# Hybrid decoder step: VectorE adds a slot's index pairs before it biases the slot's score

## The chip, the cores and the metric

The kernel runs on one core of a Trainium2 chip. The metric is the device time of one execution in microseconds (us). The kernel before took 6667.58 us, the median of 3 runs (6666.86 to 6669.77).

The engines of a core that matter here: PE (TensorE, matmuls; PEld is its weight load), VectorE (DVE), ScalarE (ACT), and SP, which issues the DMAs. Each works through its own list of instructions in order and waits on semaphores for the others.

## The reference

One layer of a decoder with three attention branches over one input projection. The branch that matters here is B, sparse attention with a learned choice of keys (DSA): 4096 prompt tokens, 6 heads of 64, 8 indexer heads; each query attends to the 256 keys of highest index score.

```
dots  = einsum('nthd,nsd->ntsh', qi, ki) * IDX_DIM ** -0.5
score = einsum('ntsh,nth->nts', relu(dots), wi) * IDX_HEADS ** -0.5     # 8 indexer heads, weighted and summed
score = where(key <= query, score, -inf)
_, sel = top_k(score, 256)
s = einsum('ntkgd,ntjkd->ntkgj', q, k[sel]) * HEAD_DIM ** -0.5
o = einsum('ntkgj,ntjkd->ntkgd', softmax(s), v[sel])
```

## The kernel before

Six stages run one after the other: memory projection, token projection, window attention, sparse attention for the prompt (`attend_sparse`), attention of the sampled tokens, and output projection. The change lies in `attend_sparse`.

It goes through 32 tiles of 128 queries. Instead of gathering keys it computes all scores of a tile against all keys up to it and adds a `bias` of -1e30 at keys that aren't selected. Keys are taken in chunks of up to 512. A *slot* is one head of a tile (n) and one chunk (g); tile t has 6 x (t // 4 + 1) of them. Three streams of work are interleaved over the slots:
- the attention of tile t: a score matmul into PSUM (PE, L980), biasing it into `p_S` with its running extreme in `p_mc` (VectorE, `biased`, L1131), the exponentials (ScalarE, L1046), and two heads later the transposes (PE, L1006), their copies to `p_PT` (ScalarE, L1054) and the product with the values (PE, L1016)
- the index scores of tile t + 2: an index matmul for one indexer head and one chunk (an *item*, PE, L989), its ReLU into one of three `relu` buffers (ScalarE, L1063), and, when a pair of chunks is there, an add of the weighted pair to `p_X` over up to 1024 columns (VectorE, `add_index`, L1161 for the first head and L1164 for the others). `index_share` deals the items evenly to the slots, one or two each for the most part, so that about two slots in three have an add
- the search for the 256th largest index score of tile t + 1: 14 *parts* (`parts_here`, `part`), dealt evenly to the slots of tile t. Eight of them count how many scores lie above a trial value (L1198) and work out the next one in small operations; the others centre, mask, take the next eight, and write the new bias (L1242). Most pass over the whole row of the tile.

Score and index matmuls share four PSUM banks `SC`, which are used in turn in the order in which PE issues them. Before PE writes a bank it waits for whoever reads it out: for a score VectorE's `biased`, for an item ScalarE's ReLU (`bank`, L967). That order is PE's own per slot: transposes of two heads ago, score, items, values. ScalarE's is: copies of transposes, exponentials of the head before, ReLUs. VectorE's order per slot is the loop that the change touches: bias, inverse of a head's softmax sum (first slot of a head), adds, search parts, and at a tile's end `finish`, which looks whether the search has found all rows.

The adds of the last two tiles do not exist (there is no tile 32 or 33), and there are no parts in tile 0.

Of the kernel before, what the change touches and what calls it, by code (L numbers as in the profile page):

```python
# [747 lines left out]
def attend_sparse(nc, ins, outs, scr):  # L748
# [6 lines left out]
    def n_chunks(t):  # L755
        return t // 4 + 1
# [7 lines left out]
    def tile_of(n):  # L764
        return n // HEADS

    def slots_of(n):
        qk = n_chunks(tile_of(n)) if n < NH else 0
        return max(qk, n_chunks(tile_of(n - LOOK)) if n >= LOOK else 0)

    def index_items(t):

        return [(h, big, c) for big in range((n_chunks(t) + 1) // 2) for h in range(8)
                for c in range(2 * big, min(2 * big + 2, n_chunks(t)))]
# [13 lines left out]
    def index_share(n, g):  # L788

        t = n // HEADS + 2  # L790
        if t >= NT:
            return []
        s, ns = place[n, g]
        items = index_items(t)
        return [(t, k) for k in range(len(items) * s // ns, len(items) * (s + 1) // ns)]

    def parts_here(n, g):

        t = n // HEADS + 1
        if not 2 <= t < NT:  # L800
            return []
        s, ns = place[n, g]
        return [i for i in range(PARTS) if (i * (ns - 1) // PARTS if i < PARTS - 1 else ns - 1) == s]
# [5 lines left out]
    def ends_here(n, g):  # L809
        s, ns = place[n, g]  # L810
        return 2 <= n // HEADS + 1 < NT and s == ns - 1
# [10 lines left out]
    for n in range(NH + LOOK):  # L822
        for g in range(slots_of(n)):
# [6 lines left out]
            if asks_here(n, g):  # L830
                t = n // HEADS + 1
# [3 lines left out]
    with ExitStack() as ctx:  # L835
# [277 lines left out]
        def _(dve):  # L1113
# [10 lines left out]
            def biased(n, g):  # L1124
                t, p = tile_of(n), n % 2
                w, r = width(t, g), ring["B", n, g]
                if g == 0 and n >= 3:
                    dve.wait_ge(p_turned, first_chunk[n - 2])
                dve.wait_ge(s_ready, r + 1)
                cols = slice(512 * g, 512 * g + w)  # L1130
                dve.tensor_tensor_reduce(S[:, n % 3, cols], SC[r % 4][:, 0:w], bias[:, cols], -SCALE, -FAR,  # L1131
                                         ALU.add, ALU.min, mc[:, p, g:g + 1]).then_inc(s_biased, 1)
                if g == n_chunks(t) - 1:
                    if n >= 2:
                        dve.wait_ge(exp_done, first_exp[n - 1])
                    dve.wait_ge(s_biased, first_chunk[n + 1])
                    dve.tensor_scalar(mjunk[:, p, 0:g + 1], mc[:, p, 0:g + 1], 1.0, None, ALU.mult, ALU.min,  # L1137
                                      accum_out=negm[:, p:p + 1]).then_inc(max_ready, 1)

            def inverse(n):  # L1140
                p, pieces = n % 2, first_exp[n + 1] - first_exp[n]
                dve.wait_ge(exp_done, first_exp[n + 1])
                dve.tensor_scalar(ljunk[:, 0:pieces], lparts[:, p, 0:pieces], 1.0, None, ALU.mult, ALU.add,
                                  accum_out=lsum[:, p:p + 1]).then_inc(l_summed, 1)
                if n >= 2:
                    dve.wait_ge(o_out, n - 1)
                dve.wait_ge(l_summed, n + 1)
                dve.reciprocal(linv[:, p:p + 1], lsum[:, p:p + 1]).then_inc(inv_ready, 1)

            def add_index(t, k):  # L1150
                h, big, cc = index_items(t)[k]
                if cc != min(2 * big + 1, n_chunks(t) - 1):
                    return
                a, b = 1024 * big, min(1024 * (big + 1), P * (t + 1))
                j = first_sum[t] + 8 * big + h
                x, r, w = X[:, t % 2, a:b], relu[:, j % 3, 0:b - a], iw[:, t % 2, h:h + 1]
                if k == 0:
                    dve.wait_ge(iq_in[t % 2], 80 * (t // 2))
                dve.wait_ge(relu_done, first_item[t] + k + 1)
                if h == 0:  # L1160
                    dve.scalar_tensor_tensor(x, r, w, ties[:, a:b], ALU.mult, ALU.add).then_inc(idx_added, 1)  # L1161
                else:
                    dve.wait_ge(idx_added, j)
                    dve.scalar_tensor_tensor(x, r, w, x, ALU.mult, ALU.add).then_inc(idx_added, 1)  # L1164
# [79 lines left out]
            def all_seen():  # L1244

                dve.wait_ge(s_biased, first_chunk[HEADS])
                dve.memset(bias[:, 0:P], 0.0)
                dve.tensor_copy(bias[:, P:2 * P], causal[:, :]).then_inc(passed, 1)
                dve.wait_ge(passed, 2)

            def part(t, i):
                if i == 0:
                    centre(t)
                elif i == 1:
                    begin(t)
                elif i < 2 + COUNTS:
                    count(t, i - 2)
                else:
                    (mask, next_eight, take, make_bias)[i - 2 - COUNTS](t)
# [40 lines left out]
            def finish(t):  # L1300

                dve.wait_ge(s_ready, ring["U", t] + 1)
                dve.sem_inc(passed, 1)
                link(dve.tensor_copy(undone[:, :], SC[ring["U", t] % 4][0:1, 0:1]))
                dve.sem_inc(told, 1)
                left = dve.value_load(undone[0:1, 0:1], min_val=0, max_val=P)
                before = done[0]
                with dve.If(left > 0):
                    search_all(t)
                    dve.sem_inc(passed, 1)  # L1310
                assert done[0] - before == SLOW_STEPS, done[0] - before
                with dve.Else():
                    dve.sem_inc(step, SLOW_STEPS)
                dve.wait_ge(step, done[0])
                dve.sem_inc(picked, 1)
                assert done[0] == STEPS * (t - 1), (done[0], t)
# [3 lines left out]
            dve.wait_ge(passed, 1)  # L1320
            for n in range(NH + LOOK):
                for g in range(slots_of(n)):
                    if n < NH and g < n_chunks(tile_of(n)):
                        biased(n, g)
                    if g == 0 and n >= LOOK:
                        inverse(n - LOOK)
                    for t, k in index_share(n, g):
                        add_index(t, k)
                    for i in parts_here(n, g):
                        part(n // HEADS + 1, i)  # L1330
                    if ends_here(n, g):
                        finish(n // HEADS + 1)
                    if (n, g) == slots[0][-1]:
                        all_seen()
# [851 lines left out]
```

## Time and profile before

| | |
|---|---|
| runs | 6666.86, 6667.58, 6669.77 us |
| profiled execution | 6669.09 us, span 6667.2 us |
| PE busy | 5927.4 us, 89% of the span |
| VectorE busy | 3641.5 us, 55% |
| ScalarE busy | 2845.0 us, 43% |
| mean granted TensorE clock | 0.953 |

Busy time is an average over stages with different limits. The sparse stage lies between about 2604 and 5870 us. The granted clock is given as a share of TensorE's full clock. A wait is the idle time of an engine in front of an instruction, with the instruction that ended it.

### The profile page before, as it was taken

The page shows a single profiled execution, that of the slowest core. Times are in us where ns is not written, and L with a number is a line of the kernel's source. Part 1 is how long each engine was busy: PE and PEld are TensorE (multiplying, and loading weights), DVE is VectorE, ACT ScalarE, POOL GpSimd, SP SyncE. Part 2 cuts the span into 40 slices and gives each one's busy share as a digit, 9 for nine tenths or more (in the row PEclk, how much of TensorE's full clock was granted, in tenths as well). Part 3 has the DMA queues.
Part 4 walks back from the last instruction along what each step waited for, and adds up shares of the span by engine and source line. Part 5 has one row for each costly group of instructions (what it writes and reads, how often), then busy time and mean ns, then how long its engine had stood idle before and what let it go on. Part 6 is the DMA issues. An engine that isn't in the chain of part 4 may idle for free. (4 is left out here: it accounts for less than half of the span.)

```text
span 6667.2 us, 78452 instructions
## 1 busy us (share of the span) xinstructions
PE 5927.4 (89%) x25717; PEld 3521.4 (53%) x25717; DVE 3641.5 (55%) x9535; ACT 2845.0 (43%) x6063; POOL 91.9 (1%) x172
## 2 busy tenths in 40 slices
PE   5999999999899996778888989888988888987998
PEld 2444444444566764445555556555555556743444
DVE  1111111111355555888888888777877777363554
ACT  1222222222354554455556665655655555521332
POOL 0000000000000000000000000000000000000000
PEclk8999999999899998799999999999999999998999
DMA  3111111111500003011100000000000000032443
GB/s 129 42 49 48 44 54 42 50 48 39 152 30 27 35 27 97 25 41 32 28 8 12 12 6 6 12 6 6 6 6 6 6 3 4 14 130 95 151 155 123
DMA packets 215242, 301.89 MB, mean 45 GB/s; under 512 B 38114, under 2 KB 169890, under 8 KB 213730
## 3 DMA queue, kind: packets, MB, share of 16 engines
q1 hardware_dynamic: 202514, 256.85, 12.1%
q0 software_dynamic: 12368, 40.71, 1.6%
q8 instruction: 168, 2.75, 0.2%
q14 instruction: 192, 1.57, 0.1%
HBM read 189.98 MB, written 120.08 MB: 47 GB/s over the span
## 5 line engine op out<-in xcount | busy, mean ns | idle before, releaser
L453 PE MATMUL t_zp<-t_w,t_xT 128*128 128x512 f32 (+1 forms) x3696 | 1442.6, 551 | 42.5 <-DVE t_w L406 42.5
L989 PE MATMUL p_SC<-p_ikT,p_iq 128*128 128x512 f32 (+3 forms) x2272 | 1125.0, 600 | 302.3 <-DVE p_mc L1131 301.4
L1016 PEld LDWEIGHTS p_OP<-p_bv,p_PT 128*128 128x128 f32 x6336 | 881.5, 200 | 396.9 <-issue 352.9
L453 PEld LDWEIGHTS t_zp<-t_w,t_xT 128*128 128x128 f32 x3696 | 662.2, 192 | 778.1 <-issue 735.2
L1063 ACT ACTIVATE p_relu<-p_SC 128x512 f32<-128x512 f32 (+3 forms) x1136 | 628.3, 565 | 750.0 <-PE p_SC L989 647.8
L980 PE MATMUL p_SC<-p_bkT,p_bq 128*128 128x512 f32 (+3 forms) x1728 | 860.7, 581 | 60.1 <-DVE p_mc L1131 59.8
L989 PEld LDWEIGHTS p_SC<-p_ikT,p_iq 128*128 128x128 f32 x2272 | 430.8, 200 | 865.9 <-DVE p_mc L1131 467.2
L1016 PE MATMUL p_OP<-p_bv,p_PT 128*128 128x64 f32 x6336 | 844.3, 277 | 10.1 <-ACT p_PT L1054 9.9
L1131 DVE CUSTOM_DVE_ANT_0 p_S<-p_SC,p_bias 128x512 f32<-128x512 f32 (+3 forms) x864 | 553.1, 645 | 311.7 <-PE p_SC L980 245.4
L288 ACT ACTIVATE t_z<-t_zp,t_rstd 128x512 f32<-128x512 f32 (+1 forms) x231 | 146.6, 635 | 1309.8 <-PE t_zp L453 1309.8
L1164 DVE SCALAR_TENSOR_TENSOR p_X<-p_relu,p_iw,p_X 128x1024 f32<-128x1024 f32 (+7 forms) x546 | 608.3, 1114 | 175.8 <-ACT p_relu L1063 167.1
L1054 ACT ACTIVATE p_PT<-p_TP 128x512 f32<-128x512 f32 (+3 forms) x864 | 485.4, 562 | 480.1 <-PE p_TP L1006 478.4
L1198 DVE TENSOR_SCALAR_CACHE_REDUCE p_Y<-p_X,p_col 128x384 bf16<-128x384 f32 (+29 forms) x240 | 609.6, 2540 | 1.0 <-issue 0.3
L1046 ACT ACTIVATE p_S<-p_S,p_negm 128x1024 f32<-128x1024 f32 (+7 forms) x480 | 477.8, 996 | 138.7 <-DVE p_mjunk L1137 101.3
L1006 PE MATMUL p_TP<-p_ident,p_S 128*128 128x128 f32 x3168 | 513.0, 282 | 18.9 <-ACT p_S L1046 18.8
L710 ACT ACTIVATE w_S<-w_S,w_o 128x256 f32<-128x256 f32 (+1 forms) x704 | 338.7, 482 | 416.7 <-DVE w_o L676 416.7
L2062 PE MATMUL f_zp<-f_w,f_mixT 128*128 128x512 f32 x1056 | 470.9, 605 | 0.0
L1006 PEld LDWEIGHTS p_TP<-p_ident,p_S 128*128 128x128 f32 x3168 | 400.0, 162 | 27.4 <-ACT p_S L1046 20.8
L685 DVE COPY w_PT<-w_TP 128x512 f32<-128x512 f32 (+1 forms) x352 | 226.6, 644 | 263.6 <-PE w_TP L620 263.2
L638 PEld LDWEIGHTS w_OP<-w_v,w_PT 128*128 128x128 f32 x2052 | 250.6, 191 | 158.5 <-DVE w_PT L685 158.5
L2062 PEld LDWEIGHTS f_zp<-f_w,f_mixT 128*128 128x128 f32 x1056 | 203.6, 196 | 244.9 <-issue 244.9
L386 DVE COPY t_qT<-t_tp 128x512 f32<-128x512 f32 (+1 forms) x132 | 81.4, 654 | 447.8 <-PE t_tp L439 447.2
(250 smaller groups left out, 5312.1 us busy)
## 6 DMA issues: line engine op xcount, KB each, us to landing
scr_qkT<-t_qT SPq DMA_DIRECT2D x33, 960.0 KB, 3.7
scr_part<-w_o POOLq DMA_DIRECT2D x96, 198.0 KB, 2.2
f_part<-scr_part SPq DMA_DIRECT2D x32, 594.0 KB, 4.7
t_x<-in_x_prompt SPq DMA_DIRECT2D x32, 512.0 KB, 3.7
f_gate<-scr_gate SPq DMA_DIRECT2D x32, 512.0 KB, 7.3
f_x<-in_x_prompt SPq DMA_DIRECT2D x32, 512.0 KB, 3.3
out_y_p<-f_y POOLq DMA_DIRECT2D x32, 512.0 KB, 6.5
p_iq<-scr_qkT SPq DMA_DIRECT2D x120, 128.0 KB, 2.8
```

Source lines behind the costliest of these rows:

```text
L453: mm = pe.matmul(zp[(NZ * p + c) % 2][:, 0:n], xT[:, p, k, :], w[:, k, a:a + n], start=(k == 0), stop=(k == KD - 1))
L980: pe.matmul(bank(ring["B", n, g])[:, 0:w], bq[:, t % 2, n % HEADS, :], bkT[:, 512 * g:512 * g + w], start=True, stop=True).then_inc(s_read ...
L989: pe.matmul(bank(ring["I", t, k])[:, 0:w], iq[:, t % 2, h, :], ikT[:, 512 * c:512 * c + w], start=True, stop=True).then_inc(s_ready, 1)
L1006: mm = pe.transpose(TP[m % 2][:, b, :], S[:, n % 3, c0:c0 + P], ident[:, :])
L1016: mm = pe.matmul(OP[n % 2][:, 0:HD], PT[:, m % 2, b, :], bv[:, 4 * g + b, s * HD:(s + 1) * HD], start=(g == 0 and b == 0), stop=(last and ...
L1046: act.activation(S[:, n % 3, a:b], S[:, n % 3, a:b], ACT.Exp, scale=-1.0, bias=negm[:, p:p + 1], accum_out=lparts[:, p, big:big + 1]).then ...
L1054: act.activation(PT[:, m % 2, 0:nb, :], TP[m % 2][:, 0:nb, :], ACT.Copy).then_inc(pT_ready, 1)
L1063: act.activation(relu[:, j % 3, 512 * (c % 2):512 * (c % 2) + w], SC[r % 4][:, 0:w], ACT.Relu, scale=0.5)\
L1131: dve.tensor_tensor_reduce(S[:, n % 3, cols], SC[r % 4][:, 0:w], bias[:, cols], -SCALE, -FAR, ALU.add, ALU.min, mc[:, p, g:g + 1]).then_in ...
L1164: dve.scalar_tensor_tensor(x, r, w, x, ALU.mult, ALU.add).then_inc(idx_added, 1)
L1198: link(dve.tensor_scalar(G[:, 0:L], X[:, t % 2, 0:L], c(W + 1), None, ALU.is_gt, ALU.add, accum_out=c(CNT)))
L2062: mm = pe.matmul(zp[2 * p + i][:, :], mixT[:, p, k * P:(k + 1) * P], w[:, k, i * 512:(i + 1) * 512], start=(k == 0), stop=(k == KD - 1))
```

## The change

In VectorE's loop over the slots the adds come ahead of the bias and the inverse; parts and the rest stay behind them.

```
             for n in range(NH + LOOK):
                 for g in range(slots_of(n)):
+                    for t, k in index_share(n, g):
+                        add_index(t, k)
                     if n < NH and g < n_chunks(tile_of(n)):
                         biased(n, g)
                     if g == 0 and n >= LOOK:
                         inverse(n - LOOK)
-                    for t, k in index_share(n, g):
-                        add_index(t, k)
                     for i in parts_here(n, g):
                         part(n // HEADS + 1, i)
```

The lists of the other engines stay as they are. On VectorE, in tile 23 (keys up to 3200 are counted for tile 24), between two counts that stand two slots apart, the kernel before has:

```order
L1223 SCALAR_TENSOR_TENSOR p_col<-p_col,p_signs 128x2
L1131 ISA p_S,p_mc<-p_SC,p_bias 128x512
L1131 ISA p_mc 128x1
L1164 SCALAR_TENSOR_TENSOR p_X<-p_relu,p_iw,p_X 128x1024
L1131 ISA p_S,p_mc<-p_SC,p_bias 128x512
L1131 ISA p_mc 128x1
L1137 TENSOR_SCALAR p_mjunk,p_negm<-p_mc 128x6
L1164 SCALAR_TENSOR_TENSOR p_X<-p_relu,p_iw,p_X 128x1024
L1198 TENSOR_SCALAR p_Y,p_col<-p_X,p_col 128x3200
```

The same place in the changed kernel (L1223 is the end of one count, L1198 the start of the next):

```order
L1223 SCALAR_TENSOR_TENSOR p_col<-p_col,p_signs 128x2
L1164 SCALAR_TENSOR_TENSOR p_X<-p_relu,p_iw,p_X 128x1024
L1131 ISA p_S,p_mc<-p_SC,p_bias 128x512
L1131 ISA p_mc 128x1
L1164 SCALAR_TENSOR_TENSOR p_X<-p_relu,p_iw,p_X 128x1024
L1131 ISA p_S,p_mc<-p_SC,p_bias 128x512
L1131 ISA p_mc 128x1
L1137 TENSOR_SCALAR p_mjunk,p_negm<-p_mc 128x6
L1198 TENSOR_SCALAR p_Y,p_col<-p_X,p_col 128x3200
```

Behind the first count the add (L1164) now precedes the bias (L1131); in front of the second count the bias and the head's extreme (L1137) now stand between add and count.

Behind that second count the next slot has no add, and is the first of a head. In the kernel before VectorE has there:

```order
L1223 SCALAR_TENSOR_TENSOR p_col<-p_col,p_signs 128x2
L1131 ISA p_S,p_mc<-p_SC,p_bias 128x512
L1131 ISA p_mc 128x1
L1143 TENSOR_SCALAR p_ljunk,p_lsum<-p_lparts 128x3
L1148 RECIPROCAL p_linv<-p_lsum 128x1
L1131 ISA p_S,p_mc<-p_SC,p_bias 128x512
L1131 ISA p_mc 128x1
L1164 SCALAR_TENSOR_TENSOR p_X<-p_relu,p_iw,p_X 128x1024
```

And in the changed kernel, at the same place:

```order
L1223 SCALAR_TENSOR_TENSOR p_col<-p_col,p_signs 128x2
L1131 ISA p_S,p_mc<-p_SC,p_bias 128x512
L1131 ISA p_mc 128x1
L1143 TENSOR_SCALAR p_ljunk,p_lsum<-p_lparts 128x3
L1148 RECIPROCAL p_linv<-p_lsum 128x1
L1164 SCALAR_TENSOR_TENSOR p_X<-p_relu,p_iw,p_X 128x1024
L1131 ISA p_S,p_mc<-p_SC,p_bias 128x512
L1131 ISA p_mc 128x1
```

The bias behind the count stays first, and only in the slot after it do add and bias change places.

## Rows read from the trace of the kernel before

**Rows 1.** VectorE's timeline (start, us long, instruction): where tiles 11 and 21 end.
```profile
3239.24 1.02 DVE L1242 TENSOR_SCALAR p_bias<-p_Y 128x1664 bf16<-128x1664 f32 x1
...
4165.78 1.62 DVE L1242 TENSOR_SCALAR p_bias<-p_Y 128x2816 bf16<-128x2816 f32 x1
```

**Rows 2.** Busy us (and instructions) of each engine, granted clock, DMA, by stretch.
```profile
2604.00:3239.00 635.00, 496.68 (x2118) 310.65 (x2117) 535.87 (x1820) 327.00 (x723) 0.00 (x0) 0.89 0.14 39
3239.00:4166.00 927.00, 834.70 (x3970) 534.22 (x3968) 769.96 (x1822) 553.99 (x1015) 0.00 (x0) 0.96 0.04 11
4166.00:5575.00 1409.00, 1261.09 (x5975) 810.47 (x5974) 1074.62 (x2140) 819.99 (x1417) 0.00 (x0) 0.96 0.02 7
```

**Rows 3.** PE's waits (total us, times, longest) in these three stretches, in turn.
```profile
PE p_SC L989 <- DVE p_mc L1131: 106.1, 50, 5.2
PE p_SC L980 <- DVE p_mc L1131: 16.0, 7, 7.7
...
PE p_SC L989 <- DVE p_mc L1131: 86.3, 57, 4.1
PE p_SC L980 <- DVE p_mc L1131: 5.8, 9, 1.2
...
PE p_SC L989 <- DVE p_mc L1131: 109.0, 61, 4.1
PE p_SC L980 <- DVE p_mc L1131: 34.2, 25, 2.5
```

**Rows 4.** PE's waits from 2604 to 5575 us, the next largest.
```profile
PE p_TP L1006 <- ACT p_S L1046: 18.8, 8, 4.8
```

**Rows 5.** VectorE's waits from 2604 to 5575 us, for ReLUs.
```profile
DVE p_X L1164 <- ACT p_relu L1063: 167.1, 192, 2.9
```

**Rows 6.** Timeline from 4500 us: start, us long, engine, instruction [idle before <- who ended it].
```profile
4500.77 0.69 DVE L1131 CUSTOM_DVE_ANT_0 p_S<-p_SC,p_bias 128x512 f32<-128x512 f32 x1 [3.20 <-PE p_SC L980]
...
4502.32 1.28 DVE L1164 SCALAR_TENSOR_TENSOR p_X<-p_relu,p_iw,p_X 128x1024 f32<-128x1024 f32 x1 [0.85 <-ACT p_relu L1063]
...
4503.52 3.54 DVE L1198 TENSOR_SCALAR_CACHE_REDUCE p_Y<-p_X,p_col 128x3200 bf16<-128x3200 f32 x1
4503.57 1.88 PE L989 MATMUL p_SC<-p_ikT,p_iq 128*128 128x512 f32 x4
...
4504.98 1.17 ACT L1063 ACTIVATE p_relu<-p_SC 128x512 f32<-128x512 f32 x2 [0.29 <-issue]
...
4506.57 1.02 PE L980 MATMUL p_SC<-p_bkT,p_bq 128*128 128x512 f32 x2
...
4508.80 0.69 DVE L1131 CUSTOM_DVE_ANT_0 p_S<-p_SC,p_bias 128x512 f32<-128x512 f32 x1
...
4509.42 1.28 DVE L1164 SCALAR_TENSOR_TENSOR p_X<-p_relu,p_iw,p_X 128x1024 f32<-128x1024 f32 x1
...
4509.56 3.33 PE L989 MATMUL p_SC<-p_ikT,p_iq 128*128 128x512 f32 x4 [1.97 <-DVE p_mc L1131]
```

**Rows 7.** VectorE's groups in the three stretches, in turn: count | busy, mean ns | idle.
```profile
L1164 DVE SCALAR_TENSOR_TENSOR p_X<-p_relu,p_iw,p_X 128x1024 f32<-128x1024 f32 (+7 forms) x126 | 122.6, 973 | 11.6 <-ACT p_relu L1063 8.1 <-issue 1.0 <-DVE p_X L1164 0.5
...
L1131 DVE CUSTOM_DVE_ANT_0 p_S<-p_SC,p_bias 128x512 f32<-128x512 f32 (+3 forms) x144 | 85.0, 590 | 47.3 <-PE p_SC L980 23.1 <-DVEq L1313 10.1 <-PE p_TP L1006 4.8
...
L1164 DVE SCALAR_TENSOR_TENSOR p_X<-p_relu,p_iw,p_X 128x1024 f32<-128x1024 f32 (+7 forms) x176 | 198.5, 1128 | 50.2 <-ACT p_relu L1063 47.7
...
L1131 DVE CUSTOM_DVE_ANT_0 p_S<-p_SC,p_bias 128x512 f32<-128x512 f32 (+3 forms) x252 | 161.2, 641 | 49.7 <-PE p_SC L980 25.6 <-DVEq L1313 17.6 <-DVE p_col L1203 1.1
...
L1164 DVE SCALAR_TENSOR_TENSOR p_X<-p_relu,p_iw,p_X 128x1024 f32<-128x1024 f32 (+7 forms) x245 | 288.3, 1177 | 114.8 <-ACT p_relu L1063 112.1
...
L1131 DVE CUSTOM_DVE_ANT_0 p_S<-p_SC,p_bias 128x512 f32<-128x512 f32 (+3 forms) x372 | 242.8, 658 | 136.6 <-PE p_SC L980 122.4 <-DVEq L1313 6.5 <-DVE p_col L1203 1.8
```

**Rows 8.** ScalarE's waits from 2604 to 5575 us, for a free ReLU buffer.
```profile
ACT p_relu L1063 <- DVE p_X L1164: 83.3, 53, 3.9
```

More of the change, by code:

```diff
@@ L1322, in _ @@
                 for g in range(slots_of(n)):
+                    for t, k in index_share(n, g):
+                        add_index(t, k)
                     if n < NH and g < n_chunks(tile_of(n)):
@@ L1326, in _ @@
                         inverse(n - LOOK)
-                    for t, k in index_share(n, g):
-                        add_index(t, k)
                     for i in parts_here(n, g):
```

## The prediction, made before the changed kernel ran

> **What bounds the kernel now.** I looked first for the stretch that the edit can reach: only the DSA stage (`attend_sparse`), and in it only tiles whose slots carry index work, that is from 2604 us to 5575 us, 2971 us of the span of 6667.2 us. The bias table of a tile is written at the end of the tile before; two of these ends cut the stretch in three [rows 1]: tiles 0 to 11, 12 to 21, and 22 to 29. Then I asked what each engine does there [rows 2]: PE is busy for 78, 90 and 90% of the three, VectorE for 84, 83 and 76%. Neither is idle enough to be out of the question, and neither is full: they hold each other up.
>
> Where, the waits tell. PE waits for `p_mc` of L1131, the biasing of a score, because the score's PSUM bank comes free only with it: 122.1 us in 57 waits, 92.1 in 66 and 143.2 in 86 [rows 3], 357 us in 209 waits. PE's only other wait of note, on ScalarE's exponentials, is 18.8 us [rows 4]. VectorE for its part waits 167.1 us for ReLUs in front of its adds [rows 5]. So the clock of the stage is a loop: PE fills the four banks, VectorE must bias a score to free one, and PE starts only as far ahead as the ring allows.
>
> One turn of that loop is in [rows 6]. At 4500.77 VectorE biases a score as soon as it is there. At 4502.32 it adds the slot's pair, 0.85 us after it ran dry, when the ReLU is done. From 4503.52 it counts (3.54 us, then eight small operations) and comes back at 4508.80. Meanwhile PE has done the next slot's score and two items (from 4503.57), and the score of the slot after (from 4506.57), and is stuck for 1.97 us until the bias of 4508.80 frees a bank at 4509.4; its item starts at 4509.56. Both ReLUs of that next slot were done at 4506.15 (4504.98 + 1.17), so at 4508.80 bias and add were both possible, and the kernel takes the one PE waits for.
>
> **The change, part by part.** No instruction is added or removed and no DMA is issued by VectorE here; PE's, ScalarE's and SP's lists are the same. In each of the 582 slots that by `index_share` have both a score and an add, the bias moves behind the add; with it moves the inverse of a softmax sum, in the first slot of a head. Two things follow around each search part.
>
> *Next slot.* After a part VectorE now adds first if the next slot has an add. In the turn above the add's step is 4503.52 - 4502.32 = 1.20 us: PE's bank comes free that much later.
>
> *Own slot.* If the slot of the part has an add itself, the bias that used to run while the ReLU was made now stands between add and part: 4509.42 - 4508.80 = 0.62 us. The part starts and ends that much later.
>
> For this turn both hold: 1.97 us become about 3.8. Now count them. The formulas of `index_share` and `parts_here` give, for the three stretches, 118, 140 and 112 slots with a part; 98, 100 and 86 of these have an add of their own; behind 99, 100 and 66 the next slot has one. With the mean durations of [rows 7] (bias 590, 641, 658 ns; add 973, 1128, 1177 ns):
> - tiles 0 to 11: 98 x 0.590 + 99 x 0.973 = 154 us
> - tiles 12 to 21: 100 x 0.641 + 100 x 1.128 = 177 us
> - tiles 22 to 29: 86 x 0.658 + 66 x 1.177 = 134 us
>
> 465 us would be it if every part held PE up. PE waited 57, 66 and 86 times for 118, 140 and 112 parts, 48, 47 and 77%, so 74, 83 and 103 us. In the first stretch nearly every slot has a part (118 in 138 slots), VectorE is the busiest engine, and an engine that sets the pace itself loses nothing by another order of work that is ready: I take half, 37 us. Waits: 37 + 83 + 103 = 223 us. Bounds: 0 (all hidden behind VectorE's own work) and 465.
>
> *Slots without a part.* In the 298 others with an add the bias goes from the moment the score is there to after ReLU and add; in the turn above from 4500.77 to 4503.52, when PE's next items want to start at 4503.57: about 0.6 us late if they need just that bank. Bounds 0 and 298 x 0.62 = 185 us; I take 0, since these slots are the ones in which the ring had room, and what PE waits there it waits less at the next part.
>
> *The clock.* After the wait of 1.97 us the two items took 3.33 us, against 1.88 us for the two before [rows 6]: half speed, the 1.2 GHz level against 2.4. The granted clock is 0.89 in the first stretch, where PE's waits are thickest (122.1 us in 635), and 0.96 in the two others (235.3 us in 2336) [rows 2, 3]. If these two fell all the way to 0.89, PE's 2095.8 busy us there would grow by 0.96/0.89, 165 us; if nothing changed, 0. No row shows how far it falls with 186 us more of waits. I take a fall to 0.93, a little under half of the way: 2095.8 x (0.96/0.93 - 1) = 68, of which I keep 60, since VectorE sets the pace part of the time. In the Trainium skill, "TensorE: Matmul & The Clock Gate", section "A second HAM failure mode: psum-queue depth-cycling", a kernel that cycles through PSUM banks with short idle spells between its matmuls swings between the two clock levels and loses throughput by it; the trace agrees, with the 3.33 us against 1.88.
>
> *Sum.* 223 + 60 = 283 us on the profiled execution's 6669.09 us (1.9 around the span) is 6952; that execution was 1.5 us over the median of the runs, so 6950 us.
>
> **Rivals.**
> *The order is hidden.* The same work is done by the same engine, bias and add are both ready behind a part, and VectorE is busy for some 80%. If it is the pace-setter throughout, PE's longer waits cost nothing: 6667.6 us, or up to 90 us more with the late tiles alone. For it: the first stretch. Against it: in tiles 22 to 29 VectorE is busy for only 76% and 86 of 112 parts do hold PE up. A rule of the Trainium skill points this way ("Perfetto Trace Analysis", section "Matmuls"): let matmul groups rotate through several PSUM banks, so that emptying one overlaps the next group's matmuls. With four score banks the time would be as before by it. The trace disagrees: four banks leave 209 waits, 357 us.
> *The other side: faster.* ScalarE waits 83.3 us for an add to free one of three ReLU buffers [rows 8]; its PT copies and exponentials queue behind these ReLUs. The adds now come a bias earlier. If these waits went and PE had been slowed by them, it would be 6667.6 - 83 = 6584 us. It decides only if PE waits for ScalarE; it does so for 18.8 us [rows 4], so I hold it unlikely.
> *Full price.* Every part holds PE up, the add-only slots do too, and the clock falls to 0.89: 465 + 185 + 165 = 815, 7480 us. For it: each longer wait delays the items, their ReLUs and so the next add, so the loop may lengthen by more than the sum. Against it: both engines' slack takes up some.
>
> **How the numbers follow.** The forecast (223 us of waits and some clock) holds for 90 to 520 us: 6760 to 7190 us, chance 0.80. Hidden, less than 90 us: 0.10, of which 0.04 within 0.2% (13 us, about what can be told from no change). Above 7190: 0.06. Faster: 0.04. So faster 0.04, same 0.04, slower 0.92. The range 6760 to 7190 leaves out 0.2.
>
> **What would show it.** PE's waits on `p_mc` should go from 357 us to some 540, the mean of a wait from 1.7 to over 2.2 us, with VectorE's rows count, add, bias in front of them. VectorE's idle time before L1131 for the score should all but go (the add waits in front of it), and that before L1164 for ReLUs grow. VectorE's and ScalarE's busy time should stay; the granted clock of tiles 12 to 29 should fall to about 0.92. Tiles 30 and 31, and all other stages, should not move. It is wrong if PE's waits grow and the span does not (hidden), or if PE's waits on `p_mc` do not grow.

## The result: 6% slower

The changed kernel took 7088.28 us (median of 4 runs, 7076.07 to 7094.64) against 6667.22 us for the kernel before (4 runs): 421 us more, ratio 1.0629 with a 95% interval of 1.0611 to 1.0647. The forecast was 6950 us, with a range of 6760 to 7190. The profiled execution took 7076.07 us, its span 7074.2 us, 407 us more than before.

The same three stretches of the sparse stage as in [rows 2], cut at the ends of the same tiles (columns as there). One label has to be set right: the second cut is where the bias of 2816 keys is written [rows 1], 22 x 128, which is tile 21's, so it is the end of tile 20. The stretches are tiles 0 to 11, 12 to 20 and 21 to 29, here as before.

```profile
2605.00:3291.00 686.00, 512.31 (x2117) 312.37 (x2117) 533.46 (x1821) 330.81 (x725) 0.00 (x0) 0.89 0.13 36
3291.00:4352.00 1061.00, 887.03 (x3967) 548.47 (x3966) 765.36 (x1821) 558.04 (x1016) 0.00 (x0) 0.93 0.03 10
4352.00:5990.00 1638.00, 1347.23 (x5980) 838.53 (x5980) 1066.64 (x2141) 825.79 (x1416) 0.00 (x0) 0.92 0.02 6
```

They grew by 51, 134 and 229 us (686, 1061 and 1638 against 635, 927 and 1409). VectorE and ScalarE do the same work in the same busy time: 533, 765 and 1067 us of VectorE against 536, 770 and 1075. PE's busy time for the same instructions rose by 16, 52 and 86 us, 154 in all, and the granted clock fell from 0.96 to 0.93 and 0.92 in the last two. Tile 30 takes 120 us and tile 31 113 us, as before.

PE's waits in the three stretches, answering [rows 3]:

```profile
PE p_SC L989 <- DVE p_mc L1131: 130.3, 74, 6.3
PE p_SC L980 <- DVE p_mc L1131: 22.6, 15, 6.3
...
PE p_SC L989 <- DVE p_mc L1131: 165.6, 118, 4.9
PE p_SC L980 <- DVE p_mc L1131: 7.2, 12, 1.1
...
PE p_SC L989 <- DVE p_mc L1131: 254.1, 152, 5.8
PE p_SC L980 <- DVE p_mc L1131: 33.1, 32, 2.1
```

Together 613 us in 403 waits, against 357 us in 209: 256 us more. With the 154 us of longer PE work these are 410 us, what the three stretches grew by (414) and, within a few us, the span (407). The mean wait did not grow (1.5 us against 1.7); there are twice as many. PE's waits on ScalarE, answering [rows 4], stayed: 18.2 us for exponentials against 18.8. So the extreme and the inverse, which move along with the bias, do not reach PE by way of ScalarE.

VectorE's and ScalarE's waits from 2605 to 5990 us, answering [rows 5], [rows 7] and [rows 8]:

```profile
DVE p_X L1164 <- ACT p_relu L1063: 643.7, 279, 7.6
...
DVE p_S L1131 <- PE p_SC L980: 16.2, 10, 3.5
```

```profile
ACT p_relu L1063 <- DVE p_X L1164: 13.3, 7, 2.9
```

VectorE used to wait for a score in front of the bias (23.1, 25.6 and 122.4 us in the three stretches, [rows 7], 171 in all); now that is 16.2 us, and it waits for ReLUs in front of the add that stands there, 643.7 us against 167.1. Of the adds directly behind another slot's bias, extreme or inverse (315 in the timeline of the stage) 263 waited, 652 us in all, L1161 included; of the 266 directly behind a part 49 did, 66 us.

Two turns of the loop (start, us long, engine, instruction, idle before it). The first is the turn of [rows 6], the fifth count of tile 23:

```profile
4746.27 3.54 DVE L1198 TENSOR_SCALAR_CACHE_REDUCE p_Y<-p_X,p_col 128x3200 bf16<-128x3200 f32 x1
...
4748.70 1.02 PE L980 MATMUL p_SC<-p_bkT,p_bq 128*128 128x512 f32 x2
...
4751.55 1.28 DVE L1164 SCALAR_TENSOR_TENSOR p_X<-p_relu,p_iw,p_X 128x1024 f32<-128x1024 f32 x1
4752.75 0.68 DVE L1131 CUSTOM_DVE_ANT_0 p_S<-p_SC,p_bias 128x512 f32<-128x512 f32 x1
...
4753.50 3.78 PE L989 MATMUL p_SC<-p_ikT,p_iq 128*128 128x512 f32 x4 [3.77 <-DVE p_mc L1131]
```

The count ends, the add goes first (4751.55), and PE has waited 3.77 us for its bank where it had waited 1.97: 1.8 us more, as the forecast had it for this turn (about 3.8). The two items behind the wait take 3.78 us, against 3.33 behind the shorter one.

The second is in tile 24, in a slot that has no part and does not stand behind one:

```profile
4861.50 1.02 PE L980 MATMUL p_SC<-p_bkT,p_bq 128*128 128x512 f32 x2
...
4866.35 1.28 DVE L1164 SCALAR_TENSOR_TENSOR p_X<-p_relu,p_iw,p_X 128x1024 f32<-128x1024 f32 x1 [1.79 <-ACT p_relu L1063]
...
4867.55 0.68 DVE L1131 CUSTOM_DVE_ANT_0 p_S<-p_SC,p_bias 128x512 f32<-128x512 f32 x1
...
4868.30 1.12 PE L989 MATMUL p_SC<-p_ikT,p_iq 128*128 128x512 f32 x2 [2.00 <-DVE p_mc L1131]
```

This one the forecast had at nothing. PE runs ahead: the score that this bias reads was done at 4862.52 (4861.50 + 1.02). VectorE is free from 4864.56 (4866.35 - 1.79), but it waits 1.79 us for the ReLU of the slot's item, adds, and begins the bias 3 us after it could have, at 4867.55. PE's next item has waited 2.00 us for the bank that this bias frees.

### The profile page after: what moved, and what is told of

It reads as the page before. It is cut to its first block and busy times, and to the rows that moved or that the text cites. A ratio compares the mean times of both kernels' runs of the same rounds, so it can differ in the third digit from the quotient of the medians.

```text
span 7074.2 us, 78309 instructions
## 1 busy us (share of the span) xinstructions
PE 6078.1 (86%) x25717; PEld 3563.8 (50%) x25717; DVE 3624.2 (51%) x9535; ACT 2857.4 (40%) x6063; POOL 91.9 (1%) x172
## 5 line engine op out<-in xcount | busy, mean ns | idle before, releaser
L989 PE MATMUL p_SC<-p_ikT,p_iq 128*128 128x512 f32 (+3 forms) x2272 | 1186.3, 623 | 552.8 <-DVE p_mc L1131 549.9
L1016 PEld LDWEIGHTS p_OP<-p_bv,p_PT 128*128 128x128 f32 x6336 | 908.1, 206 | 411.4 <-issue 374.0
L1164 DVE SCALAR_TENSOR_TENSOR p_X<-p_relu,p_iw,p_X 128x1024 f32<-128x1024 f32 (+7 forms) x546 | 608.9, 1115 | 699.4 <-ACT p_relu L1063 643.7
L980 PE MATMUL p_SC<-p_bkT,p_bq 128*128 128x512 f32 (+3 forms) x1728 | 889.1, 598 | 66.9 <-DVE p_mc L1131 66.7
L1016 PE MATMUL p_OP<-p_bv,p_PT 128*128 128x64 f32 x6336 | 869.0, 282 | 9.7 <-ACT p_PT L1054 9.6
L1131 DVE CUSTOM_DVE_ANT_0 p_S<-p_SC,p_bias 128x512 f32<-128x512 f32 (+3 forms) x864 | 548.2, 641 | 137.4 <-PE p_SC L980 89.7
L1198 DVE TENSOR_SCALAR_CACHE_REDUCE p_Y<-p_X,p_col 128x384 bf16<-128x384 f32 (+29 forms) x240 | 609.5, 2539 | 0.7
L1006 PE MATMUL p_TP<-p_ident,p_S 128*128 128x128 f32 x3168 | 532.0, 290 | 18.3 <-ACT p_S L1046 18.2
L1006 PEld LDWEIGHTS p_TP<-p_ident,p_S 128*128 128x128 f32 x3168 | 417.0, 167 | 27.9 <-ACT p_S L1046 20.6
L980 PEld LDWEIGHTS p_SC<-p_bkT,p_bq 128*128 128x128 f32 x1728 | 283.0, 206 | 84.7 <-DVE p_mc L1131 64.4
```

The source lines that it names most:

```text
L980: pe.matmul(bank(ring["B", n, g])[:, 0:w], bq[:, t % 2, n % HEADS, :], bkT[:, 512 * g:512 * g + w], start=True, stop=True).then_inc(s_read ...
L989: pe.matmul(bank(ring["I", t, k])[:, 0:w], iq[:, t % 2, h, :], ikT[:, 512 * c:512 * c + w], start=True, stop=True).then_inc(s_ready, 1)
L1006: mm = pe.transpose(TP[m % 2][:, b, :], S[:, n % 3, c0:c0 + P], ident[:, :])
L1016: mm = pe.matmul(OP[n % 2][:, 0:HD], PT[:, m % 2, b, :], bv[:, 4 * g + b, s * HD:(s + 1) * HD], start=(g == 0 and b == 0), stop=(last and ...
L1198: link(dve.tensor_scalar(G[:, 0:L], X[:, t % 2, 0:L], c(W + 1), None, ALU.is_gt, ALU.add, accum_out=c(CNT)))
```

## Experiments

Theory: PE's pace is set by how soon VectorE frees a score bank, so whatever stands between a score's arrival and the next bank's release costs time: the ReLU wait, the add, the part. Rivals: only the length of the add behind a part counts; or a bias that waits for a ReLU is all that costs; or ScalarE's buffers.

**The change in one class of slots at a time.** Where `first` holds, the adds go ahead of the bias, elsewhere they stay behind:

```
+                    first = follows_part(n, g)        # or: parts_here(n, g) and not follows_part(n, g)
+                                                      # or: neither of the two
+                    if first:
+                        for t, k in index_share(n, g):
+                            add_index(t, k)
                     (bias, inverse)
-                    for t, k in index_share(n, g):
-                        add_index(t, k)
+                    if not first:
+                        for t, k in index_share(n, g):
+                            add_index(t, k)
```

> Adds ahead of the bias only in the 265 slots that stand right behind a slot with a search part; in all others the order of before. If what costs is the add between a part's end and the bias that frees the bank (the forecast's term for the next slot), most of the loss is here: some 190 of the 421 us. If what costs is the bias waiting behind a ReLU, little is here, since behind a part the ReLUs are done: under 120 us.

Measured 6903.84 us against 6668.73 (ratio 1.0356, 1.0339 to 1.0373): +235 us. ReLUs are mostly done there (of 265 adds behind a part 46 waited, 68 us in all), so here it is the add's length, on top of the ReLU wait and the add that stand ahead of the part.

> Adds ahead of the bias only in the 183 slots that have a part and do not stand behind one. By the forecast's term (the part starts one bias later, 0.6 us, three times in four or fewer) about 70 us of waits and some clock: 100 us. If the bias that waits for the ReLU is the cost, PE stalls here too before the part has begun: 150 to 200 us.

Measured 6797.3 us (1.0195, 1.0178 to 1.0212): +129 us, between the two expectations.

> Adds ahead of the bias only in the 134 slots that neither have a part nor stand behind one. The forecast put these at 0 (PE has room in the ring there): within 20 us of before. If the bias that waits for the ReLU is the cost, 134 times about 0.6 us and more with the clock: 80 to 150 us.

Measured 6726.16 us (1.0083, 1.0065 to 1.01): +57 us, where the forecast had 0: between the two expectations. PE's waits on the bias in these three kernels are 515, 449 and 407 us against 361 in the whole of before. The last one:

```profile
PE p_SC L989 <- DVE p_mc L1131: 345.7, 219, 7.3
PE p_SC L980 <- DVE p_mc L1131: 61.6, 49, 6.1
```

235 + 129 + 57 = 421 us: the three classes add up to the whole loss. The add behind a part is the largest piece; the other two classes hold 186 us.

The timelines also say what stands on VectorE directly ahead of the bias that ends a wait of PE over the whole execution (number of waits, us in all):

| kernel | a part | an add that stands behind a part | any other add |
|---|---|---|---|
| before | 213, 361 | none | none |
| adds first behind a part | 61, 78 | 208, 424 | 5, 13 |
| adds first in slots with a part | 209, 371 | none | 112, 79 |
| adds first in slots without | 214, 362 | none | 54, 46 |
| the change | 56, 71 | 206, 435 | 145, 111 |

In the kernel before, every wait is ended by the bias right behind a part. In the second and third class those waits stay as they were; what is new are short waits, about 0.7 to 0.9 us each, for a bias that stands behind an add. Most of these adds had waited for their ReLU (104 of the 112, 48 of the 54, 127 of the 145).

**The ring.** The changed kernel, then the kernel before, with five score banks; the values' output has one bank in place of two (cut: `r % 5` and `OP[0]` where the banks are used, and a wait for the output of the head before instead of the one before that).

```
-        SC = [... for i in range(4)]
+        SC = [... for i in range(5)]
-        OP = [... for i in range(2)]
+        OP = [... for i in range(1)]
-                if r >= 4:
-                    kind, count = ring_users[r - 4]
+                if r >= 5:
+                    kind, count = ring_users[r - 5]
```

> The changed kernel with five score banks in the ring instead of four; the fifth is taken from the output of the values, which has one bank instead of two. If PE's loss is its wait for a score bank, it reaches one matmul further while VectorE adds: waits on the bias fall from 617 us to 350 or less, and the time to 6750 to 6900 us. If the loss came from VectorE's or ScalarE's own order, the time stays within 50 us of 7088.

Measured 6772.33 us: 316 us less than with four banks (1.0157 of the kernel before with four).

```profile
PE p_SC L980 <- DVE p_mc L1131: 178.3, 106, 4.5
PE p_SC L989 <- DVE p_mc L1131: 139.2, 81, 8.0
PE p_OP L1016 <- ACT p_o L1091: 126.8, 78, 6.9
```

The waits on the bias are halved, 318 us against 617, though the single output bank brings a new wait of 127 us.

> The kernel before (bias first) with the same five score banks and one output bank as the changed kernel had in the run with five banks (6772 us). If the fifth bank hides most of what the order of add and bias costs, the two lie near each other: before with five banks 6600 to 6700 us, so that the order costs 70 to 170 us in place of 421. If the fifth bank merely sped up both alike, before with five banks is near 6668 - 316 = 6350 us.

Measured 6589.42 us against 6663.7 (0.9886, 0.987 to 0.9903), 74 us less, a little below the expected span. With five banks the order of add and bias costs 183 us, not 421, a little above the expected 70 to 170. The 183 make the fifth bank look better than it is: the profiled execution of this kernel took 1142 us behind tile 29, where the order of adds can change nothing, and the changed kernel with five banks 1103 (granted clock 0.90 against 0.93 there). Up to the end of tile 29 the two take 5446 and 5666 us, with four banks 5575 and 5988: the order costs 220 us in place of 413. So a bank more takes away about half of the loss. In what is left PE's waits on the bias are again the larger part: 318 us against 190.

**Taking links out of the chain.** Four kernels change what VectorE does between a score and the next bias.

```
adds last:        bias(s), inverse, parts(s), adds(s)
lag, adds first:  adds(s-1), bias(s), inverse, parts(s)
lag, adds behind: bias(s), inverse, adds(s-1), parts(s)
deferred:         bias(s), inverse, adds put off from s-1, then parts(s) with adds(s) put off,
                  or, without a part, adds(s)
```

> The other way round: in each slot bias, inverse, parts, and the adds last. The part no longer waits for the slot's ReLU, and begins at once behind the bias; the add, whose ReLU is done by then, stands between the part and the next bias. If the loop of part and bank sets the pace, the bank comes free earlier by the ReLU wait (0.85 us in the turn shown) in each of the slots with a part and an add: 50 to 150 us faster than before. Rival: ReLU buffers come free late, ScalarE's waits for them grow beyond 83 us and hold up its copies for PE: no gain, or slower.

Measured 6543.72 us (0.9804, 0.9771 to 0.9836), 125 us faster than before; VectorE's wait for ReLUs is almost gone, and ScalarE's wait for buffers (73.0 us) did not grow. The profile of this kernel:

```profile
DVE p_X L1164 <- ACT p_relu L1063: 48.3, 73, 1.7
```

Its four runs lie at 6523 to 6525 and at 6563 to 6569 us. The profiled one, of the upper pair, shows granted clocks of 0.87 and 0.85 in two stretches behind tile 29, so a part of that spread lies outside the change. Up to the end of tile 29 it takes 5446 us, 129 less than before.

> As the change, the adds stand ahead of the bias in every slot, but they are the adds of the slot before, whose ReLUs are long done. So the add's own length still stands between a part and the bias behind it, and no bias waits for a ReLU of its own slot. If the length of the add behind a part is the main cost, some 200 to 250 us of the 421 stay; if it is the wait for the ReLU, most of the loss goes: under 100 us.

Measured 6577.19 us (0.9846, 0.9817 to 0.9875). Here the adds stand ahead of the bias in every slot, as in the change, and the kernel is 92 us *faster* than before. The first expectation missed, and the second fell short: not most of the loss went, but more than all of it. The list of VectorE differs from the change only in which slot's add stands ahead of the bias, and that is worth 511 us (7088 against 6577). So the 235 us above are not a fixed price of an add behind a part.

> Bias, then the adds of the slot before, then the part. No add waits for a ReLU of its own slot, but it stands between the bias and the part. By the theory of the bank: a part begins 0.85 us earlier than in the kernel before (no ReLU wait), as in the kernel with adds last, so 6530 to 6600 us. If ReLU buffers are the limit: 6650 us or more.

Measured 6561.32 us (0.9841, 0.9825 to 0.9858), as expected. The add has the same length in all three of these kernels and stands once between two biases, ahead of the part or behind it; they lie within 34 us.

> The adds of a slot with a part are put off until behind the next slot's bias: bias, part, next bias, then both slots' adds. Nothing but the part stands between two biases there. If the bank is what PE waits for, this beats the kernel with parts first and adds last (6544 us) by another 30 to 100 us: about 6480 us. Rival: three ReLU buffers are too few for adds so late, ScalarE waits for them and holds up its copies: 6550 to 6700 us.

Measured 6517.37 us (0.977, 0.9754 to 0.9786): the fastest of these kernels, 151 us faster than before, but only 26 us ahead of the kernel with adds last, where 30 to 100 were expected. Nothing but the part stands between the two biases:

```profile
4361.02 0.68 DVE L1131 CUSTOM_DVE_ANT_0 p_S<-p_SC,p_bias 128x512 f32<-128x512 f32 x1
...
4361.63 3.41 DVE L1198 TENSOR_SCALAR_CACHE_REDUCE p_Y<-p_X,p_col 128x3072 bf16<-128x3072 f32 x1
...
4365.80 0.56 DVE L1131 CUSTOM_DVE_ANT_0 p_S<-p_SC,p_bias 128x384 f32<-128x384 f32 x1 [0.19 <-DVE p_col L1203]
4366.42 1.12 PE L989 MATMUL p_SC<-p_ikT,p_iq 128*128 128x512 f32 x2 [0.82 <-DVE p_mc L1131]
4366.64 1.28 DVE L1164 SCALAR_TENSOR_TENSOR p_X<-p_relu,p_iw,p_X 128x1024 f32<-128x1024 f32 x1
```

ScalarE's waits for ReLU buffers rose, to 105.7 us, and did not outweigh it. Of the 151 us, 94 are shorter waits of PE on the bias (361 to 267) and 57 are shorter PE busy time (5927 to 5871).

> Deferred adds (6517 us with four banks) and five score banks. PE's remaining waits on the bias there are 267 us; the fifth bank should take half of them away and the single output bank give back about 100 us of waits on ScalarE: 6450 to 6550 us. If the bank is no limit any more, slower than 6517 by the single output bank.

Measured 6545.02 us (0.982, 0.9803 to 0.9836), 28 us slower than with four banks: within the expected span, but the fifth bank is worth less here than the second output bank.

In order of what lies between two biases with a part, up to the end of tile 29, where the clock of the later stages plays no part: part alone 5423 us; add and part 5446, 5457, 5476; ReLU wait, add and part 5575 (before); the same with another add behind the part 5815 (first class). Without the ReLU wait an add costs 23 to 53 us, with it 239 for an add of the same length. That PE's own work hides more of a shorter chain fits this, but no run shows it by itself. Nor is the length between two biases the whole account: in the change too only an add stands there beside the part, and it takes 5988 us, with the bias ahead of the part held back by the ReLU and the add.

So neither of the first two rivals holds alone, since the add behind a part and the bias that waits for a ReLU both cost. ScalarE's wait for buffers is 13.3 us in the change, the slowest kernel, and 73 to 106 us in the four orders above, which are faster than before: it is not the limit.

## Why the prediction was right, and where it was short

- *What bounds the kernel* held: PE's wait for the bank. A bank more took away half of the loss, and orders of VectorE's list that free the bank sooner took away all of it and more.
- *Next slot and own slot*: 223 us of waits were forecast and 256 measured. By stretch 37, 83 and 103 were forecast; 31, 81 and 144 measured. The half that I took in the first stretch was about right. The counts of parts were for tiles 12 to 21 and 22 to 29, the waits for 12 to 20 and 21 to 29; with 126 parts in either stretch, 91 and 95 own adds, and 91 and 75 next ones the two terms come out at 84 and 103, so nothing hangs on it. The sign "some 540" left out the first stretch: 357 + 223 is 580.
- *By class* about 153 us of waits were meant to fall on slots behind a part and 70 on other slots with one. The runs gave 153 and 88 more than before. The first is right in mechanism and size. The second is right by luck: waits held by a part that starts later grew by only 9 us there, and 79 us are waits for a bias behind its add, which the forecast did not have.
- *Slots without a part*, set at 0 with a bound of 185, cost 57 us, 46 of them waits. (Of the 298 slots 164 stand behind a part and were counted there already; 134 are left.) The step that failed is the argument that "the ring had room" there. The bias waits for the ReLU of its own slot, the ReLU for an item, and the item, a bank further, for a bias: a chain that has no part in it. Its waits are short. That is why the number of waits doubled and the mean did not grow, as the prediction said it would (over 2.2 us; 1.5 measured): the waits behind part and add are 2.1 us long on average, the 145 behind other adds 0.8. It is also the main reason why the last stretch, with 100 of the 134 slots of this class, was over its term: in the run of this class alone PE's waits there are 178 us against 143.
- *The clock* fell to 0.93 and 0.92, as taken (0.93). The price was mis-sized: 60 us forecast, 154 measured as longer PE work. By the prediction's own formula the clock accounts for 2095.8 x (0.96 / 0.925 - 1) = 79 us of it; the other 75 no run explains. That VectorE's pace would hide some of it was wrong: VectorE was busy for only 72 and 65% of the two later stretches.
- *Rival, hidden*: fell with the first result. *Rival, faster by free ReLU buffers*: its first half came true, ScalarE's wait fell from 83.3 to 13.3 us, and PE gained nothing by it. *Full price* (7480 us) stayed away.

## What to carry to other kernels

When several streams share a ring of buffers, order each consumer's list by who waits for the buffer: first what frees one for the engine that sets the pace, then what only feeds a later stage. Before moving work ahead of such a release, ask what that work itself waits for: if its input comes from the engine that needs the buffer, the move closes a loop, and slots without a long operation in front pay for it too. The same look shows gains: putting the adds off behind the next release was worth 151 us.

## What was not expected of the hardware

Five score banks in place of four, with one output bank less, made the changed kernel 316 us faster and the kernel before only 74 us (322 and 129 up to the end of tile 29). What lies behind tile 29, where no add is left, took 1081 to 1126 us in the profiles of the kernels with four banks, at granted clocks of 0.95 to 0.90; no run shows why. And PE's busy time for one and the same list of matmuls differed by 154 us between two orders of another engine's work, with granted clocks of 0.96 and 0.92 to 0.93.
